# Third modulation group of a hybrid SSD and attention backbone: from TensorE products in the SSD walk to VectorE multiply-adds between the evictions of the output projection

## What is computed

```
mod_l = (silu(c) @ ada_w[i] + ada_b[i])          # latent tokens, 6 x 1024 values for layer i
mod_c = (silu(c_ctx) @ ada_w[i] + ada_b[i])      # context tokens, the same weights
sh1, sc1, g1, sh2, sc2, g2 = split(mod_l, 6)
hl = rmsnorm(xl, norm1_g[i]) * (1.0 + sc1) + sh1  # in front of the mixer of layer i
xl = xl + g1 * mixer(hl)
hl2 = rmsnorm(xl, norm2_g[i]) * (1.0 + sc2) + sh2 # in front of the experts of layer i
```

## Time and profile before

| | before |
|---|---|
| median of 3 runs (lowest, highest) | 1293.34 us (1291.96, 1298.55) |
| the profiled execution | 1293.57 us |
| its span, first to last instruction | 1291.9 us |
| TensorE busy | 1228.3 us, 95% |
| VectorE busy | 600.8 us, 47% |
| ScalarE busy | 375.3 us, 29% |
| HBM read | 337.81 MB |

### The profile page before, as it was taken

The page is one execution under the profiler, slowest core; times in us unless marked ns, Lnnn a source line. Parts: engine busy times, 40 slices in busy tenths (PEclk is TensorE's granted clock), DMA queues, the critical chain, the costliest instruction groups (busy, mean ns, idle before and its releaser), DMA issues.

```text
span 1291.9 us, 14772 instructions
## 1 busy us (share of the span) xinstructions
PE 1228.3 (95%) x5839; PEld 581.6 (45%) x5839; DVE 600.8 (47%) x910; ACT 375.3 (29%) x707; POOL 202.3 (16%) x192
## 2 busy tenths in 40 slices
PE   5899999999999899999999998899999899999978
PEld 3344454454554444573333433343444556444322
DVE  1448486776776322481111111757665755232213
ACT  2334567676686200110010101220115621000000
POOL 1001244444344300000000001120200300000000
PEclk9999999999999899999999999899999999999999
DMA  9334445556446573289999999975247337999997
GB/s 360 117 134 155 164 144 181 196 200 224 164 135 208 194 281 147 81 343 428 424 428 427 428 427 394 392 286 200 94 170 289 141 111 301 425 428 423 427 416 287
DMA packets 79487, 347.96 MB, mean 269 GB/s; under 512 B 9554, under 2 KB 27906, under 8 KB 62642
## 3 DMA queue, kind: packets, MB, share of 16 engines
q1 hardware_dynamic: 72667, 327.62, 65.1%
q10 hardware_dynamic: 4236, 10.41, 2.1%
q0 software_dynamic: 2512, 8.97, 1.7%
HBM read 337.81 MB, written 9.17 MB: 269 GB/s over the span
## 4 chain that ended last, share of the span: by engine, by line
PE 78%; DVE 8%; DMA 4%; ACT 3%; SPq 3%; issue 2%; POOL 1%; ACTq 1%; DVEq 0%; POOLq 0%
PE psum L1804 23%; PE psum L822 10%; PE psum L833 9%; PE psum L1172 8%; PE psum L2674 6%; SPq L1776 3%; PE psum L1888 3%; PE psum L2731 2%; PE psum L342 2%; PE psum L866 2%; PE psum L886 2%; PE psum L1942 2%; PE psum L882 1%; DMA spare<-in_ada_w 1%; DMA spare<-in_moe_w_down 1%
## 5 line engine op out<-in xcount | busy, mean ns | idle before, releaser
L1804 PE MATMUL psum<-ring,arena 128*32 128x512 f32 (+2 forms) x1328 | 305.0, 595 | 9.5 <-DMA ring<-in_moe_w_gate 4.1
L1804 PEld LDWEIGHTS psum<-ring,arena 128*32 128x32 f32 (+2 forms) x1328 | 94.3, 124 | 168.7 <-issue 153.9
L822 PE MATMUL psum<-hT,ring 128*128 128x512 f32 x384 | 169.7, 596 | 0.0
L2674 PE MATMUL psum<-ring,hT 128*128 128x512 f32 x320 | 140.2, 595 | 1.6 <-DVE hT L2440 1.6
L1172 PE MATMUL psum<-ring 128*128 128x512 f32 x256 | 114.7, 605 | 4.8 <-issue 3.5
L833 PE MATMUL psum<-hT,ring 128*128 128x512 f32 x256 | 112.5, 592 | 0.0
L822 PEld LDWEIGHTS psum<-hT,ring 128*128 128x128 f32 x384 | 71.3, 190 | 85.3 <-issue 85.3
L2674 PEld LDWEIGHTS psum<-ring,hT 128*128 128x128 f32 x320 | 60.3, 191 | 75.9 <-issue 74.1
L1029 DVE SCALAR_TENSOR_TENSOR arena<-arena,X 128x512 f32<-128x512 f32 x96 | 92.8, 966 | 3.4
L1804 PE MATMUL psum<-spare,arena 128*64 128x512 f32 (+1 forms) x192 | 85.0, 594 | 0.0
L1804 PE MATMUL psum<-arena 128*32 128x512 f32 (+1 forms) x264 | 84.8, 593 | 0.0
(11 more groups left out here) (369 smaller groups left out, 1674.4 us busy)
## 6 DMA issues: line engine op xcount, KB each, us to landing
ring<-in_moe_w_up SPq DMA_DIRECT2D x20, 2048.0 KB, 16.4
ring<-in_moe_w_down SPq DMA_DIRECT2D x20, 2048.0 KB, 20.4
ring<-in_moe_w_gate SPq DMA_DIRECT2D x19, 2048.0 KB, 15.6
arena<-in_ada_w SPq DMA_DIRECT2D x36, 512.0 KB, 5.2
ring<-in_ssd_w_in SPq DMA_DIRECT2D x16, 1024.0 KB, 7.6
ring<-acs_d SPq DMA_DIRECT2D x16, 1024.0 KB, 6.8
spare<-in_ada_w SPq DMA_DIRECT2D x16, 1024.0 KB, 5.0
arena<-in_moe_w_gate SPq DMA_DIRECT2D x6, 2048.0 KB, 17.3
```

The costliest lines, as they stand in the source:

```text
L822: mm = pe.matmul(psum[:, bank, :], w_[:, k, c0:c0 + P], hT[:, k, :], start=(k == 0), stop=(k == KD - 1))
L1804: mm = pe.matmul(psum[rows, dst, :], lhsT[:, k, rows], weight(s_, a, k, part), start=(k == 0), stop=(k == a - 1))
L2674: mm = pe.matmul(psum[:, 4 + m_ % 2, :], hT[:, k, t * P:(t + 1) * P], slot(qkv_slot[n], KD)[:, k, :], start=(k == 0), stop=(k == KD - 1))
```

## The change

Group 3 (`MIDDLE`) leaves the walk. `PIECES` falls from 24 to 16 and `ada_turn` keeps turn 0 alone, one piece in each iteration. Group 3 is now computed in the manner of the late groups, but for both kinds of token: for each of its eight pieces VectorE runs two instructions (one for each kind) that accumulate into two buffers in `hT`, which is free once the last z projection is done. Pieces 0 and 1 go ahead of the gating of the walk's last block, pieces 2 and 3 ahead of the first eviction of the output projection, pieces 4 and 5 after eviction 0, piece 6 after eviction 1, piece 7 after eviction 2. SP loads the pieces into the two halves of `spare`, each when the half is free. TensorE adds the partitions with eight matmuls between output tiles 3 and 4, VectorE adds the bias, SP stores the result, and only then may SP issue the first expert weights. The silu of c is kept for both kinds of token, and the small loads of group 3's columns move behind the first expert weights.

```diff
--- before.py
+++ after.py
@@ -114,8 +114,8 @@
         arena = sb("arena", [P, ARENA])
         ident = sb("ident", [P, P])
         spare = sb("spare", [P, SLOT])
-        small = sb("small", [P, 32])
-        c_keep = small[:, 24:32]
+        small = sb("small", [P, 40])
+        c_keep = small[:, 24:40].rearrange("p (c k) -> p c k", c=2)
         psum = es.enter_context(nc.psum_tensor("psum", [P, 8, NB], F32))
         dts = sb("dts", [P, 5, 4 * 64])
         tri_up, tri_lo = X[:, 1, 768:768 + P], X[:, 1, 768 + P:D]
@@ -275,7 +275,8 @@
             act.wait_ge(pool_set, 5)
             for cond, at in ((0, CC0 + 8), (1, CC0)):
                 act.activation(c_sil[:, :, cond], cols[:, at:at + KD], ACT.Silu).then_inc(csil_ready, 1)
-            act.activation(c_keep, cols[:, CC0:CC0 + KD], ACT.Silu).then_inc(csil_ready, 1)
+            for cond, at in ((0, CC0 + 8), (1, CC0)):
+                act.activation(c_keep[:, cond, :], cols[:, at:at + KD], ACT.Silu).then_inc(csil_ready, 1)
 
 
 
@@ -293,7 +294,7 @@
 
             rows_ = ada_b.rearrange("l (q n) -> (l q) n", q=3)
             for j in range(4):
-                sp.dma_start((ada_bias[q - 1] if q <= WALKED else late_bias)[32 * j:32 * j + 32, :],
+                sp.dma_start((ada_bias[q - 1] if q <= WALKED else mid_bias if q == MIDDLE else late_bias)[32 * j:32 * j + 32, :],
                              rows_[q:q + 1, j * NB:(j + 1) * NB].broadcast_to([32, NB])).then_inc(adab_in, 16)
 
         def keep_busy(pe, bank, n):
@@ -322,8 +323,8 @@
 
         ada_in = [sem(f"ada_piece_in{n}") for n in range(2)]
         ada_used = sem("ada_piece_used")
-        PIECES, WALKED = 3 * KD, 3
-        ADA_COPY = {5: 1, 10: 2, 15: 3}
+        PIECES, WALKED = 2 * KD, 2
+        ADA_COPY = {7: 1, 15: 2}
 
         def ada_piece_sync(sp, p):
             if p >= 2:
@@ -676,7 +677,7 @@
 
         def ada_turn(do, eng, p, i, n):
 
-            if n == 2 or (n == 1 and i % 2) or p >= PIECES:
+            if n or p >= PIECES:
                 return p
             do(eng, p)
             return p + 1
@@ -709,10 +710,14 @@
                 p = ada_turn(ada_piece_sync, sp, p, i, 1)
                 if i == NT - 3:
                     wout_load(sp, 4, 0, 0, xb_mm, NSEQ)
+                    for p_ in range(2):
+                        mid_piece_sync(sp, p_)
                 if i + 2 < NT:
                     decay_rows_sync(sp, i + 2)
                 p = ada_turn(ada_piece_sync, sp, p, i, 2)
             wout_load(sp, 5, 1, 0, z_mm, NT)
+            for p in range(2, 4):
+                mid_piece_sync(sp, p)
 
 
         def dt_tensor(pe):
@@ -1098,6 +1103,8 @@
                     conv_vector(v, step, BCN + i + 2)
                 if i + 1 < NT:
                     decay_vector(v, step, i + 1)
+            for p in range(2):
+                mid_piece_vector(v, p)
             gated_vector(v, step, NT - 1)
 
 
@@ -1187,6 +1194,7 @@
             mm.then_inc(y_scale, 1)
             for n in range(1, 2 * TT):
                 if n == TT:
+                    mid_sum_tensor(pe)
                     moe0.columns_tensor(pe)
                     for kk in range(2):
                         wait_full(pe, kk, 1)
@@ -1228,10 +1238,13 @@
                 step(v.scalar_tensor_tensor(out=tmp, in0=psum[:, wout_bank(n), :], scalar=rstd[:, t:t + 1], in1=GB[:, t // 2, part],
                                             op0=ALU.mult, op1=ALU.mult))
                 v.tensor_tensor(out=X[:, t, part], in0=X[:, t, part], in1=tmp, op=ALU.add).then_inc(wo_added, 1)
+                for p in ((4, 5), (6,), (7,))[n] if n < TT - 1 else ():
+                    mid_piece_vector(v, p)
                 if n == TT - 2:
                     moe0.norm.prepare(v, step)
                 if n == TT - 1:
                     moe0.columns_vector(v, step)
+                    mid_copy_vector(v)
                 if half:
                     moe0.norm.tile_mid(v, step, t)
                     if t < TT - 1:
@@ -2517,7 +2530,53 @@
 
         late_bias, late_mod = carve(arena, 16384, NB), carve(arena, 16384 + NB, NB)
         late_acc = Xflat[:, 0:2 * D]
-        LATE = 2 * KD
+        LATE, MIDDLE = 2 * KD, WALKED + 1
+        BEFORE_LATE = PIECES + 2 * KD
+        mid_acc = [hflat[:, 2 * D * cd:2 * D * (cd + 1)] for cd in range(2)]
+        mid_bias, mid_mod = carve(arena, 12288, NB), [carve(arena, 12288 + NB * (cd + 1), NB) for cd in range(2)]
+
+        def mid_piece_sync(sp, p):
+
+            if p >= 2:
+                sp.wait_ge(ada_used, PIECES + 2 * p - 2)
+            sp.dma_start(late_buf(p), ada_w[1, p * P:(p + 1) * P, 0:2 * D]).then_inc(ada_in[p % 2], 16)
+
+        def mid_piece_vector(v, p):
+
+            if p == 0:
+                v.wait_ge(z_mm, NT)
+                v.wait_ge(csil_ready, 4)
+            v.wait_ge(ada_in[p % 2], 32 * (PIECES // 2) + 16 * (p // 2) + 16)
+            for cd in range(2):
+                col, n = c_keep[:, cd, p:p + 1], PIECES + 2 * p + cd
+                if p == 0:
+                    v.tensor_scalar(mid_acc[cd], late_buf(p), col, None, ALU.mult).then_inc(ada_used, 1)
+                else:
+                    v.wait_ge(ada_used, n - 1)
+                    v.scalar_tensor_tensor(out=mid_acc[cd], in0=late_buf(p), scalar=col, in1=mid_acc[cd], op0=ALU.mult,
+                                           op1=ALU.add).then_inc(ada_used, 1)
+
+        def mid_sum_tensor(pe):
+
+            pe.wait_ge(ada_used, PIECES + 2 * KD)
+            for cd, bank in ((0, 6), (1, 1)):
+                for j in range(4):
+                    m = pe.matmul(psum[32 * j:32 * j + 32, bank, :], small[:, 16:17].broadcast_to([P, 32]), mid_acc[cd][:, j * NB:(j + 1) * NB],
+                                  start=True, stop=True)
+            m.then_inc(ada_done, 1)
+
+        def mid_copy_vector(v):
+
+            v.wait_ge(ada_done, 2)
+            v.wait_ge(adab_in, 16 + 64 * MIDDLE)
+            for cd, bank in ((0, 6), (1, 1)):
+                v.tensor_tensor(out=mid_mod[cd], in0=psum[:, bank, :], in1=mid_bias, op=ALU.add).then_inc(ada_copied, 1)
+
+        def mid_store_sync(sp):
+
+            for cd in range(2):
+                sp.wait_ge(ada_copied, MIDDLE + 1 + cd)
+                sp.dma_start(mod_d[MIDDLE, cd, :].rearrange("(j n) -> j n", j=4), mid_mod[cd][0:97:32, :]).then_inc(mod_out, 16)
 
...
@@ -2941,13 +2998,20 @@
             group_weights_sync(sp)
             fused_sync(sp)
             wout_sync(sp)
+            for p in range(4, 6):
+                mid_piece_sync(sp, p)
             moe0.norm.load(sp, lambda e: None)
             moe0.router_load(sp)
+            ada_bias_sync(sp, MIDDLE)
             att_small_sync(sp)
+            for p in range(6, KD):
+                mid_piece_sync(sp, p)
+            mid_store_sync(sp)
+            stored = [(moe0.row_stored[j], 16 * (TT // 2)) for j in range(2)]
+            moe0.sync_first(sp, 0, ([(ada_used, BEFORE_LATE)], [(wo_mm, TT)], [], [(wo_mm, 2 * TT)], [], [(wo_mm, 2 * TT + 1)], []))
+            moe0.sync_first(sp, SLOTS + 1, ([moe0.scored()], stored + [(moe0.s["h_T_mm"], 2)]))
+            sp.wait_ge(mod_out, 32 * MIDDLE)
             mod_b_sync(sp)
-            stored = [(moe0.row_stored[j], 16 * (TT // 2)) for j in range(2)]
-            moe0.sync_first(sp, 0, ([], [(wo_mm, TT)], [], [(wo_mm, 2 * TT)], [], [(wo_mm, 2 * TT + 1)], []))
-            moe0.sync_first(sp, SLOTS + 1, ([moe0.scored()], stored + [(moe0.s["h_T_mm"], 2)]))
             moe0.sync_rest(sp)
             sp.wait_ge(*moe0.used(*moe0.holder[NINTH]))
             sp.wait_ge(*moe0.routed("LAST"))
...
```

More of the change, by code:

```diff
@@ L2561, in late_copy_vector @@
         def late_copy_vector(v, q, bank):
-            n = q - WALKED
-            v.wait_ge(ada_done, n + 1)
+            n = q - MIDDLE
+            v.wait_ge(ada_done, n + 2)
             v.wait_ge(adab_in, 16 + 64 * q)
             if n > 1:
-                v.wait_ge(mod_out, 32 * WALKED + 16 * (n - 1))
+                v.wait_ge(mod_out, 32 * MIDDLE + 16 * (n - 1))
             v.tensor_tensor(out=late_mod, in0=psum[:, bank, :], in1=late_bias, op=ALU.add).then_inc(ada_copied, 1)
@@ L2597, in att_sync @@
                 if p == 2:
-                    ada_bias_sync(sp, WALKED + 1)
+                    ada_bias_sync(sp, MIDDLE + 1)
                 if p == LATE - 1:
-                    late_store_sync(sp, WALKED + 1)
-                    ada_bias_sync(sp, WALKED + 2)
-            moe1.sync_first(sp, 0, ([(ada_used, PIECES + LATE)],))
-            late_store_sync(sp, WALKED + 2)
-            sp.wait_ge(mod_out, 32 * WALKED + 32)
+                    late_store_sync(sp, MIDDLE + 1)
+                    ada_bias_sync(sp, MIDDLE + 2)
+            moe1.sync_first(sp, 0, ([(ada_used, BEFORE_LATE + LATE)],))
+            late_store_sync(sp, MIDDLE + 2)
+            sp.wait_ge(mod_out, 32 * MIDDLE + 32)
             sp.wait_ge(A["T_mm"], 12)
@@ L2686, in att_tensor @@
             pe.wait_ge(A["qkv_copied"], len(QKV))
```

(6 more changed lines are left out.)

28 lines of the change are left out of this document (13 added, 15 removed).

## The result

| | before | after |
|---|---|---|
| median (lowest, highest), 20 runs each | 1293.27 us (1290.73, 1298.55) | 1297.88 us (1295.18, 1303.57) |
| the profiled execution | 1293.57 us | 1296.35 us |
| its span | 1291.9 us | 1294.7 us |

The ratio after to before is 1.003, with a 95% interval of 1.002 to 1.0041: the change costs 0.3%, about 4 us, where 2.5 us were forecast as gained. The median lies 0.4 us above the upper end of the range.

A forecast was written before the change was run, and what follows sets the result against it. The prediction took TensorE to bound the walk. From 1293.57 us, -7.0 + 0 + 1.8 + 2.0 + 0.7 + 0 = -2.5 gave 1291.1 us, with a range of the whole of 1287.5 to 1297.5.

The forecast's parts named there:

- The walk: Even iterations 0 to 14 each lose a 1.00 us piece on TensorE; seven of eight pay: 7.0 us gained.
- My test of the odd iterations: Iteration 13, already without turn 1, had 2.4 us in hand at the outputs; even iterations should become like it.
- Wait for slot 5: After the states of iteration 15 TensorE arrives 1.0 us sooner and waits 1.0 us longer: 3.1 us.
- End of the walk: VectorE's pieces 0 and 1, 7.3 us, fit its 7.7 us gap ahead of the gating: 0 us, bounds 0 and 1.0.
- Tile 3: Output projection: x lands at 465, eviction 1 ends about 478.8, so TensorE waits 1.8 us; bounds 0 and 5.
- The order of a ring by itself: DMA descriptors taken strictly in issue order would land x at 467, with a wait of nearly 4 us; not adopted.
- The sum waits for pieces 6 and 7: Ahead of the summing matmuls TensorE waits 0.7 us; 0 without SP's hold-up, 5.6 us with it.
- given back at the sum: Rival, chance 0.17: SP is held up as before and the sum waits 5.6 us: +2.4, 1296.0 us.
- a sign of being wrong: The prediction is wrong if the waits of tile 3 and of the sum add up to over 6 us.
- The sums: Eight summing matmuls on TensorE's path, two sums at full clock: 2.0 us, bounds 2.0 and 3.9.
- The clock: A single 1.8 us wait in dense matmuls should not lower TensorE's clock: 0 us, bounds 0 and 2.1.

The follow-up runs named there:

- the three edits: Changed kernel with pieces 6 and 7 loaded ahead of the router's tables, piece 5 behind eviction 1, ScalarE's copy ahead of its decays: 0.9942, 1288.25 us.

## Why the prediction was wrong, by its steps

**The walk: -7.0 forecast, -7.2 measured, partly for other reasons.** Seven pieces of 1.00 us are gone. In addition the kernel before had a wait of 1.44 us in iteration 14, which I had not read:

```profile
408.52 7.11 PE L1172 MATMUL psum<-ring 128*128 128x512 f32 x16 [1.44 <-issue]
```

It is gone too. Against it, the last iterations became 19.28, 19.54, 19.56 and 19.54 us long instead of 19.16, 1.3 us in all. -7.0 - 1.44 + 1.28 is -7.2. That the forecast came so near is luck: two terms that it didn't have cancel. TensorE's z projections of the changed kernel:

```profile
372.01 7.03 PE L838 MATMUL psum<-hT,ring 128*128 128x512 f32 x16
...
391.57 7.03 PE L838 MATMUL psum<-hT,ring 128*128 128x512 f32 x16
```

They are 19.56 us apart, and so is what ScalarE and VectorE do for one another, decays, copy, convolution, gating, silu, decays again. ScalarE:

```profile
373.69 4.79 ACT L972 ACTIVATE ring<-ring,dts 128x128 f32<-128x128 f32 x16
378.38 0.58 ACT L938 ACTIVATE arena<-psum 128x512 f32<-128x512 f32 x1
...
389.08 0.63 ACT L946 ACTIVATE arena<-arena 128x512 f32<-128x512 f32 x1 [5.84 <-DVE arena L1081]
```

ScalarE runs at this pace long before TensorE shows it: from 213.17 us on its operation of L946 comes every 19.5 to 19.6 us, while TensorE's iterations still take 19.16. It loses 0.4 us on TensorE in each, and only the last four iterations feel it. A second bound lay 0.4 us above the new length of an iteration. My test of the odd iterations looked at the margin of the outputs in one of them, 2.4 us. A loop whose round takes 19.54 us hides behind iterations of 20.16 and 19.16 us, because their mean is 19.66. The copy ahead of the decays removed it after the change and gained nothing in the walk before it; that is shown.

**Wait for slot 5: 3.1 forecast, 3.08 measured.** The wait is set by the last z projection and 7.8 us of loading. I had taken it as fixed; the exchange of two steps in iteration 14 takes it away. In the kernel before that brought 4 us (0.9986 to 0.9954), in the changed one nothing that can be told from none, because the gating then waits.

**End of the walk: 0 forecast (bounds 0 and 1.0), 1.2 measured.** The gap was to begin at 426.35 on the changed kernel's clock (1.0 us sooner, less the 7.0 of the walk); VectorE came at 428.16, because its loop had not become shorter with TensorE's. The gating starts at 435.07, where the outputs were done at about 433.8. In the other traces with the walk of the changed kernel and low clock behind slot 5 the outputs end some 1.7 us later, and the gating is in time.

**Tile 3: 1.8 forecast, 1.88 measured**, and x released the first eviction at 459.36, which is 465.3 on the time scale of before; 465 was forecast. The order of a ring by itself (the Trainium skill, DMA: Bandwidth & Descriptors, Queues, rings and completion order) had given 467 and a wait of nearly 4 us; the trace doesn't show it.

**The sum waits for pieces 6 and 7: 0.7 forecast, 4.92 measured. This is the step that failed.** The prediction says "The queue will be less full than before when SP gets there, so I take 0.7". It had worked out both ends: 0 without SP's hold-up and 5.6 with it. The row showed 9.83 us, and I reasoned it away with a guess on the queue that no row bore out. It became 11.48, and 11.05 in the kernel without pieces 2 to 7. The rival "given back at the sum" is what happened; with the 1.88 us of tile 3 the two waits add up to 6.8 us, over the 6 that the prediction gave as a sign of being wrong. Shown is that the place of the two loads in SP's list is the cause: with them moved ahead of the tables the wait is gone, and 6 us with it. The share of the hold-up follows from the rows and has no run of its own: without it SP would have been through the small transfers at about 462.4 (473.83 less 11.48), before piece 6's half of `spare` was free at 466.3.

**The sums: 2.0 forecast (bounds 2.0 and 3.9), 3.64 measured.** Behind a wait of 4.92 us the granted clock is at its low level. Stretches of the kernel after, around the sums (columns as in the earlier trace rows):

```profile
491.00:495.00 4.00, 3.83 (x18) 0.78 (x18) 3.90 (x5) 0.00 (x0) 0.00 (x0) 0.50 0.00 0
495.00:516.00 21.00, 21.00 (x49) 9.43 (x49) 8.17 (x15) 1.15 (x2) 0.76 (x2) 0.98 0.74 300
```

0.50 is 1.2 GHz. This was in the bounds, but it is not a term of its own: whoever takes the long wait must take the slow sum with it. The rival added 5.6 and kept 2.0.

**The clock: 0 forecast at tile 3, and none measured.** After its wait of 1.88 us the 32 records take 14.00 us, which is full clock. The Trainium skill, TensorE: Matmul & The Clock Gate, section HAM oscillation, tells of a kernel in which the clock falls in every wait for data; its waits are longer than this one, so it isn't at odds with the trace. In this kernel's trace the clock stays at full behind 1.88 us and is low behind 4.92.

**The sum of it, made anew.** -7.2 (walk), +1.2 (gating), +1.9 (tile 3), +4.9 (wait of the sum), +3.6 (sum) and -0.4 (tiles 1 to 3, 43.60 us for 96 records instead of 44.01) give +4.0; the table above has +4.1. The forecast for the same place was -2.5. Of the difference of 6.6 us, 4.2 are the wait of the sum, 1.6 its clock and 1.2 the gating, less 0.4 for tiles 1 to 3.

## What to carry to other kernels

A load that is needed soon should not stand behind small tables in the list of an engine that issues in order, while megabytes are under way: if a row shows the issuing engine held there, take that length as the forecast, not as the worst case, and price the clock behind the wait with the wait. When work is taken off the engine that bounds a loop, work out the length of the next loop round (here 19.54 against 19.16 us), and not the slack at one place. And before work is moved to another engine, look whether the waits that stand around it can be taken away where it is: here that brought 6 of the 8 us (0.9954 without the move, 0.9939 with it).

## What was not expected of the hardware

**The clock behind a wait of 3 us.** Twelve records took 5.39 us behind the wait for slot 5 in the kernel before (2.08 us), in the changed kernel (3.08) and with the loads early (3.07), but 8.29 with the copy first (2.99), 7.08 with the three edits (3.02) and 7.08 in the kernel before with the copy first (2.06). With pieces 0 and 1 only, with the router's weights last and with the sum one tile later they took 7.08 or 7.09 (3.05, 2.96 and 2.99), though these kernels are the changed one up to there, instruction for instruction. So neither the length of the wait nor the kernel's own instructions decide it alone; one execution was profiled of each, and what decides is open. Where no low clock fell into the 96 records of tiles 1 to 3 they took 41.45 us, and otherwise 43.1 to 44.5. A difference of 2 us between two traces can be this and nothing else.

**GpSimd beside VectorE's multiply-adds.** While these ran in the kernel after, from 441.04 on, three small GpSimd operations took a multiple of their time (1.02, 0.31 and 0.20 us before):

```profile
441.20 3.07 POOL L1150 TENSOR_TENSOR small<-small 128x4 f32<-128x4 f32 x1 [2.20 <-DVE small L1227]
...
445.84 2.25 POOL L1510 CAST arena<-arena 128x128 f32<-128x128 int32 x1
448.04 2.24 POOL L1511 CAST arena<-arena 128x4 f32<-128x4 int32 x1
```

About 2 us more for each, a little under the 2.35 us of one multiply-add. The Trainium skill, SBUF — State Buffer, section Who interferes with whom, calls the port pair of the two engines "an exclusive lock", and has a VectorE instruction with two inputs in SBUF keep out a GpSimd instruction that reads SBUF, not one that only writes it. These durations fit that, and so does it that the operations between them that only write (IOTA and MEMSET) took no longer than before. Nothing waited for them here.
